# Modulation vectors of a transformer block: shift and scale made among the attention's units, the gate around the selection, loads in that order

## The chip, the cores and the metric

The kernel runs on one core of a Trainium2 chip. The metric is the device time of one execution in microseconds; the runs shown are of the whole program, inputs in HBM, result written back to HBM. Its engines are TensorE (PE; PEld is its weight load), VectorE (DVE), ScalarE (ACT), GpSimd (POOL) and SyncE (SP), which here only issues DMAs. Each engine runs its own list of instructions in order; semaphores order them against each other.

## The reference

A first block (gated recurrence and a dilated attention) is followed by a second block of two layers. All of it is float32. The second block is what the change touches, cut to its shape here:

```python
for i in range(2):
    m  = (silu(c)     @ w_ada[i] + b_ada[i]).reshape(1, 1, 6, 1024)   # six vectors for the 512 tokens
    mc = (silu(c_ctx) @ w_ada[i] + b_ada[i]).reshape(6, 1024)         # and for the 256 context tokens
    h  = rmsnorm(x) * g * (1 + m[1]) + m[0]                           # shift 0, scale 1
    y  = even_mixer(...) if i == 0 else odd_mixer(...)                # attention and projection
    x  = x + m[2] * y                                                 # gate 2
    h  = rmsnorm(x) * g2 * (1 + m[4]) + m[3]                          # shift 3, scale 4
    x  = x + m[5] * ec_moe(h)                                         # gate 5
# ec_moe: softmax over 16 experts; each expert takes its 64 best tokens (32 of the context);
#         y = (silu(xs @ w_gate) * (xs @ w_up)) @ w_down, times the router's value, added back
```

In layer 0 the same is done for the context, with `mc`. Layer 1 is the last and has no context behind its attention. `w_ada[i]` is 1024 x 6144, so each of the six vectors is a product of two rows (token and context) with a 1024 x 1024 matrix of 4 MB; each expert's three matrices are 4 MB each, 16 experts a layer.

## The kernel before

The program is written once per engine. `tensor()`, `vector()`, `scalar()`, `gpsimd()` and `sync()` list the stages in order: first block, `even` projection of layer 0, attention `ea` (24 differential pairs, 48 units), attention `eb` (48 units), output projection `oute`, `moe(0)`, the `odd` projection, attention `o` (64 units), output projection `outo`, `moe(1)`.

Weights pass through slots of 16 KB a partition in the arena `AR`: slots 0 and 1 are always free for them, slots 2 to 5 lie over the memory of the stages and slot 6 over the residual rows. `LOADS` is one list in the order in which SyncE issues the loads, 2 MB each as a rule; `sync()` walks it. Before it issues a load it waits until the slot's last content has been used (`slot_freed`) and, for some keys, for more. SyncE also writes the normalised rows (`h_rows`) and residual rows (`x_rows` or `out`) to HBM in `sp_moe`, and reads `x_rows` back before the `odd` norm. Because SyncE runs in order, a wait for one slot holds all loads behind it.

A vector `(l, j)` (layer, number; layer -1 is the first block) is made in these steps. `pe_ada_mm` multiplies the two input rows with one half of the matrix: eight matmuls of 512 columns with weights 32 wide, in turn in the four column groups of the array (L407). `dve_ada_row` copies the half to `RB1` (L440), or adds the bias where the vector is a gate (L438, `j` 2 or 5). `pe_ada_end` then turns the row into columns with eight small matmuls (L426), or, for a gate, spreads it over the partitions with matmuls against `sel` (L421), and `dve_ada_end` writes the columns to `MC` and `MG` (L467, L475) or the gate to `GB` (L454). `RB1` is one buffer, so the vectors are made one after the other.

In the first attention (`AT1`) such work already runs as fill: `Attn` takes a list of items, spread over its units, and each engine runs the items of unit `i` four steps later. `fine(l, j)` cuts a vector into eight items of two matmuls, an empty item and `ada_end`. `pe_attn`, `dve_attn` and `act_attn` serve `ea`; `pe_pairs` and its like serve `eb` and `o`, where the fill holds the `up` groups of the next heads. In both, `pe_scores` is L632, the turn of the probabilities L643, the product with the values L667 or L843, the maximum L732, the exponential L687.

`moe(l)` before: PE makes vectors 3 and 4 (`pe_ada(l, 3)`, `pe_ada(l, 4)`), turns the normalised rows and routes them (L541, L1826), serves the selection (`pe_topk`; the selection itself is a row of `max`, `max_index` and `match_replace` on DVE, L1896 to L1900), makes vector 5, turns the indices (`pe_idx`), in layer 0 makes vector 0 of layer 1, and goes to the experts. DVE has the same order: norm, 3, 4, `dve_hT`, `dve_topk`, 5, `dve_idx` (L1918 to L1926), and `dve_ada(1, 0)` in layer 0. GpSimd gathers an expert's rows (L2234) once the indices are there and scatters the result with an add (L2247). In layer 0 every weight is split into two parts first (ACT L1943, DVE L1951, matmuls L1985); in layer 1 the matmuls read it as it is (L2170).

Of the kernel before, what the change touches and what calls it, by code (L numbers as in the profile page):

```python
# [153 lines left out]
def program(nc, T, out, known):  # L154
    ctx = ExitStack()
    with ctx:
# [4 lines left out]
        K = Banks(P, C)  # L161
# [92 lines left out]
        def colchunk(key, w, n0, n1, slots):  # L254
            cyc(key, w[:, n0:n1].rearrange("(c p) n -> p c n", p=128), (w.shape[0] // 128, n1 - n0), slots)

        three, two, four, six = [0, 1, 2], [0, 1], [0, 1, 2, 6], [0, 1, 2, 3, 4, 5]

# [26 lines left out]
        for i, (a, b) in enumerate(EVEN_CH):  # L285
            colchunk(("even", i), T["w_in_even_2"][0], a, b, two)
        for i in range(2):
            colchunk(("oute", i), T["w_out_even_2"][0], i * 512, i * 512 + 512, two)
        ada_loads(0, [3, 4], two)
        ada_loads(0, [5], three)  # L290
        ada_loads(1, [0], three)
        expert_loads(0)
        ada_loads(1, [1, 2], three)
        colchunk(("odd",), T["w_in_odd_2"][0], 0, 416, two)
        add(("qup",), T["w_q_up_2"][0].rearrange("(c p) n -> p c n", p=128), (2, 1536), 0)
        add(("kvup",), T["w_kv_up_2"][0], (1, 2048), 1)
        rr[0] = 0
        for i in range(2):
            colchunk(("outo", i), T["w_out_odd_2"][0], i * 512, i * 512 + 512, two)
        ada_loads(1, [3, 4], two)  # L300
        ada_loads(1, [5], three)
        expert_loads(1)
# [347 lines left out]
        def pe_attn(A, fill=None):  # L650
            n = len(A.units)
            for step in range(n + 4):
                if step < n:
                    pe_scores(A, step)
                i = step - 2
                if 0 <= i < n and not A.units[i].get("skip"):
                    pe_turn_p(A, i)
                i = step - 3
                if 0 <= i < n and not A.units[i].get("skip"):
                    u = A.units[i]  # L660
                    nn = u["nk"] // 128
                    b = K.fill(6 + (i // 2 if A.mixed else i) % 2, "pv", A.tag, i)
                    P.wait_ge("read", "tr", A.tag, i)
                    u["vready"](P)
                    ptc = A.Pt[i % len(A.Pt)]
                    for k in range(nn):
                        m = pe.matmul(bank(b)[:, 0:128], ptc[:, 128 * k:128 * k + 128], u["v"](k), start=(k == 0),  # L667
                                      stop=(k == nn - 1))
                    m.then_inc(*K.full("pv", A.tag, i))
                i = step - 4  # L670
                if 0 <= i < n:
                    for it in A.fill[i]:
                        fill(it)
# [1036 lines left out]
        for j in range(6):  # L1710
            k0, nk = (0, 768) if j < 4 else (512, 256)
            for h in range(4):
                for c in range(2):
# [3 lines left out]
                                      out=O6[:, j, 128 * h:128 * h + 128], skip=(c == 0), mix=(c == 1)))  # L1717
        ATA = Attn("ea", units, Pb4, PTb)
        units = []
# [14 lines left out]

        def pe_fillB(it):
            pass

# [193 lines left out]
        def act_split(l, i):  # L1931
            if i >= len(PIECES[l]):
                return
            key, hf = PIECES[l][i]
            if i < 3:
                S.wait_ge("full", MLAST[l], 1, OUTP[MLAST[l]] - 1)
            elif i < 4:
                S.wait_ge("xw", l)
                S.wait_ge("read", MLAST[l], 1, OUTP[MLAST[l]] - 1)
            else:  # L1940
                S.wait_ge("used", l, i - 4)
            weight_wait(S, key)
            s.copy(pair(i)[0], raw_half(key, hf)).then_inc(*S.up("hi", l, i))  # L1943
# [327 lines left out]
        def dve_moe(l):  # L2271
            tag = f"m{l}"
            res_wait(V, MLAST[l])
            dve_norm(tag)
            dve_ada(l, 3)
            dve_ada(l, 4)
            dve_hT(tag)
            dve_topk(l)
            dve_ada(l, 5)
            dve_idx(l)  # L2280
            if l == 0:
                dve_ada(1, 0)
            dve_experts1() if l else dve_experts(l)

        def pe_moe(l):
            pe_ada(l, 3, 7)
            pe_ada(l, 4, 6)
            pe_route(l)
            pe_topk(l)
            pe_ada(l, 5, 7)  # L2290
            pe_idx(l)
            if l == 0:
                pe_ada(1, 0, 7)
            pe_experts1() if l else pe_experts(l)
# [279 lines left out]
        for gi in range(4):  # L2574
# [13 lines left out]
            if gi < 3:  # L2588
                for i in range(13):
                    fills.setdefault(max(0, 16 * gi - 2 + i), []).append(("up", gi + 1, i))  # L2590
        ATO = Attn("o", units, Pb4, [GB[0], GB[2], GB[3]], fills=fills, Rb=RbA)
        norm_mem("m1")


        def tensor():
# [13 lines left out]
            pe_even()  # L2609
            pe_attn(ATA)  # L2610
            pe_pairs(ATB, pe_fillB)
            pe_oute()
            pe_moe(0)
            pe_ada(1, 1, 6)
            pe_ada(1, 2, 7)
            pe_hT("no")
            pe_odd()
            for i in range(13):
                pe_up(0, i)
            pe_pairs(ATO, lambda it: pe_up(it[1], it[2]))  # L2620
            P.wait_ge("read", "pv", "o", 63)
# [3 lines left out]
        def vector():  # L2625
# [24 lines left out]
            V.wait_ge("full", "hturn", *HTS[-1])  # L2650
            dve_attn(ATA)
            V.wait_ge("full", "pv", "ea", 47)
# [3 lines left out]
            dve_outproj("oute", OT, gsc, tmps, 0)  # L2656
            dve_moe(0)
            dve_ada(1, 1)
            V.wait_ge("xr", 0)
# [5 lines left out]
            for i in range(13):  # L2665
                dve_up(0, i)
            dve_pairs(ATO, lambda it: dve_up(it[1], it[2]))
            dve_outproj("outo", OT4, None, tmps, 1)
            dve_moe(1)

        def scalar():
# [24 lines left out]
            S.wait_ge("full", "even", 4, 5)  # L2696
            act_attn(ATA)
            S.wait_ge("full", "pv", "ea", 47)
# [10 lines left out]
            for i in range(13):  # L2709
                act_up(0, i)  # L2710
            act_pairs(ATO, lambda it: act_up(it[1], it[2]))
            act_outproj("outo", OT4, None)
            act_moe(1)

        def gpsimd():
# [9 lines left out]
            for i in range(13):  # L2725
                pool_up(0, i)
            pool_pairs(ATO, lambda it: pool_up(it[1], it[2]))
            pool_outproj("outo", tmps)
            pool_experts(1)

        def sync():
            for i, (key, src) in enumerate(LOADS):
# [4 lines left out]
                if key[0] == "ada" and key[3] == 1 and key[2] in (2, 5):  # L2737
                    sp_bias(key[1], key[2])
                if key == ("ada", 1, 0, 1):
                    sp_moe(0)  # L2740
                if key == ("gate", 1, 0, 1):
                    sp_moe(1)
                if key == ("ada", 1, 2, 1):
                    Q.wait_ge("scat", 0, 15)
                    sp.dma_start(XALL, T["x_rows"].rearrange("(j p) d -> p j d", p=128))\
                        .then_inc(*Q.up("xr", 0, by=16))
                if slot == 2 and key[0:2] in (("ada", 0), ("ada", 1)) or key[0:2] in (("gate", 0), ("up", 0)):
                    Q.wait_ge("full", "oute", 1, 5)
                if slot == 6:
                    Q.wait_ge("xw", 0)  # L2750
                if slot >= 2 and key[0:3] == ("ada", 1, 5) or key[0:2] in (("gate", 1), ("up", 1)):
                    Q.wait_ge("full", "pv", "o", 63)
# [46 lines left out]
```

## Time and profile before

| | us |
|---|---|
| median of 3 runs (2689.45 to 2700.64) | 2689.82 |
| profiled execution, its own time | 2695.25 |
| its span in the profile | 2693.7 |
| PE busy in the span | 2309.2 (86%) |
| DVE busy | 1314.5 (49%) |
| ACT busy | 982.1 (36%) |

The page's line on the chain that ended last gives PE 50%, DVE 18%, DMA 17%, ACT 9% and "issue" 5% of the span. Where the stages lie in the profiled execution, by the starts of their rows:

| stage | from | to |
|---|---|---|
| attention `ea` | 636 | 750 |
| attention `eb` | 750 | 868 |
| projection `oute` | 868 | 951 |
| between, layer 0 | 951 | 1055 |
| experts of layer 0 | 1055 | 1640 |
| between the layers, `odd` | 1640 | 1767 |
| attention `o` | 1767 | 2056 |
| projection `outo` | 2056 | 2111 |
| between, layer 1 | 2111 | 2191 |
| experts of layer 1 | 2191 | 2694 |

A row of a timeline or a chain begins with its start and its duration in us; what stands in square brackets is the idle time of that engine before it and who ended it. An idle engine costs nothing unless it is on the chain.

### The profile page before, as it was taken

Reading aid. Unit: us, or ns where it says so; the run is one execution under the profiler, and the core shown is the slowest. Engines: PE = TensorE matmul, PEld = TensorE weight load, DVE = VectorE, ACT = ScalarE, POOL = GpSimd, SP = SyncE. Lnnn points to the kernel's source line nnn. Section 1 sums busy time; section 2 is a strip of 40 time slices with the busy share of each in tenths; the row PEclk is TensorE's granted clock in tenths of the full one; section 3 lists DMA queues with packets and bytes.
Section 4 is the critical chain, followed back from the end, with each engine's and each line's share of the span. In section 5 each row is a group of like instructions: output and inputs, shape, how many; then the busy total and the mean of one; then the engine's idle time right before and its main releaser. Section 6 shows DMA issues by size and latency. Waiting matters only on the chain.

```text
span 2693.7 us, 26540 instructions
## 1 busy us (share of the span) xinstructions
PE 2309.2 (86%) x10239; PEld 1279.2 (47%) x10239; DVE 1314.5 (49%) x2428; ACT 982.1 (36%) x1612; POOL 389.3 (14%) x324
## 2 busy tenths in 40 slices
PE   4998987999899985999999996778889868777787
PEld 2444533446666433666676663445555322222222
DVE  2147525536864135998888893466663131111111
ACT  2014333214554024888888872244442100000000
POOL 0000000000111100255445520000001001000000
PEclk9999998999999977999999996889999879999999
DMA  7113501101000077999999986000010689999998
GB/s 261 63 63 107 184 22 67 63 16 63 1 1 2 31 282 288 337 372 365 369 380 372 373 347 232 18 1 1 1 63 13 244 343 400 402 402 405 406 412 343
DMA packets 92347, 546.31 MB, mean 203 GB/s; under 512 B 7711, under 2 KB 10543, under 8 KB 67518
## 3 DMA queue, kind: packets, MB, share of 16 engines
q1 hardware_dynamic: 81806, 518.95, 49.2%
q0 software_dynamic: 6144, 20.98, 3.4%
q10 hardware_dynamic: 4272, 4.69, 0.5%
q8 instruction: 82, 1.34, 0.2%
q14 instruction: 43, 0.35, 0.0%
HBM read 523.62 MB, written 20.97 MB: 202 GB/s over the span
## 4 chain that ended last, share of the span: by engine, by line
PE 50%; DVE 18%; DMA 17%; ACT 9%; issue 5%; ACTq 0%; POOL 0%; SPq 0%; DVEq 0%; POOLq 0%
DMA AR<-in_w_exp_gate_dram 13%; PE PS L1610 7%; DVE RW L1951 6%; PE PS L632 6%; PE PS L930 5%; PE PS L1985 5%; PE PS L2170 4%; PE PS L643 3%; ACT AR L2039 3%; PE PS L1317 3%; ACT RW L1943 2%; PE PS L1151 2%; PE PS L843 2%; PE PS L407 2%; PE PS L667 1%
## 5 line engine op out<-in xcount | busy, mean ns | idle before, releaser
L1951 DVE TENSOR_TENSOR RW<-AR,RW 128x2048 fp32r<-128x2048 f32 x192 | 432.2, 2283 | 54.3 <-ACT RW L1943 54.3
L2170 PE MATMUL PS<-AR 128*64 128x512 f32 x1536 | 375.6, 636 | 94.8 <-DMA AR<-in_w_exp_gate_dram 47.4
L1943 ACT CAST RW<-AR 128x2048 fp32r<-128x2048 f32 x192 | 363.8, 1912 | 145.4 <-PE PS L1985 108.2
L1985 PE MATMUL PS<-RW,RX 128*96 128x512 f32 x1536 | 364.0, 396 | 15.7 <-DVE RX L2084 15.2
L1985 PEld LDWEIGHTS PS<-RW,RX 128*96 128x96 f32 x1536 | 248.4, 163 | 122.2 <-issue 16.3
L2170 PEld LDWEIGHTS PS<-AR 128*64 128x64 f32 x1536 | 115.0, 145 | 330.1 <-issue 261.9
L632 PE MATMUL PS<-AR 128*128 128x256 f32 (+5 forms) x640 | 243.9, 498 | 4.4 <-POOL AR L617 2.3
L1610 PE MATMUL PS<-AR 128*128 128x512 f32 (+1 forms) x480 | 193.5, 560 | 3.4 <-DMA AR<-in_w_in_even_dram 3.4
L1985 PE MATMUL PS<-RW,RA 128*96 128x512 f32 x768 | 185.4, 397 | 11.7 <-DVE RA L2118 11.7
L732 DVE TENSOR_REDUCE AR<-PS 128x1 f32<-128x768 f32 (+1 forms) x160 | 135.6, 847 | 88.4 <-PE PS L632 88.1
L2247 POOL DMA_INDIRECT x_rows<-AR x16 | 119.3, 7458 | 352.2 <-DVE AR L2128 278.0
L2234 POOL DMA_INDIRECT AR<-h_rows,AR x32 | 146.1, 4566 | 164.9 <-DVE AR L1922 77.6
L2187 ACT COPY AR<-PS 128x512 f32<-128x512 f32 x16 | 9.4, 587 | 410.4 <-PE PS L2155 410.4
L632 PEld LDWEIGHTS PS<-AR 128*128 128x128 f32 (+1 forms) x640 | 110.4, 196 | 102.2 <-issue 96.3
L687 ACT ACTIVATE AR<-PS,AR 128x768 f32<-128x768 f32 (+1 forms) x160 | 130.6, 816 | 70.4 <-DVE AR L732 28.2
L1985 PEld LDWEIGHTS PS<-RW,RA 128*96 128x96 f32 x768 | 123.1, 163 | 68.4 <-issue 17.2
L930 PE MATMUL PS<-AR 128*128 128x512 f32 x320 | 137.8, 593 | 1.1 <-DVE AR L953 0.6
L1610 PEld LDWEIGHTS PS<-AR 128*128 128x128 f32 x480 | 91.3, 194 | 93.3 <-issue 91.1
L643 PE MATMUL PS<-AR 128*128 128x128 f32 x800 | 118.0, 277 | 20.2 <-ACT AR L709 7.5
L617 POOL COPY AR<-AR 64x128 f32<-64x128 f32 x80 | 25.4, 322 | 705.3 <-ACT AR L1650 313.3
L407 PE MATMUL PS<-AR 128*32 128x512 f32 x480 | 86.7, 786 | 44.5 <-DMA AR<-in_w_ada_dram 31.2
L643 PEld LDWEIGHTS PS<-AR 128*128 128x128 f32 x800 | 94.4, 142 | 62.2 <-issue 15.9
(328 smaller groups left out, 2672.1 us busy)
## 6 DMA issues: line engine op xcount, KB each, us to landing
AR<-in_w_exp_gate_dram SPq DMA_DIRECT2D x64, 2048.0 KB, 14.2
AR<-in_w_exp_up_dram SPq DMA_DIRECT2D x64, 2048.0 KB, 11.1
AR<-in_w_exp_down_dram SPq DMA_DIRECT2D x64, 2048.0 KB, 21.8
AR<-in_w_ada_dram SPq DMA_DIRECT2D x30, 2048.0 KB, 8.2
AR<-in_w_in_dram SPq DMA_DIRECT2D x6, 2048.0 KB, 8.2
AR<-in_w_in_even_dram SPq DMA_DIRECT2D x4, 2048.0 KB, 8.2
AR<-in_w_out_dram SPq DMA_DIRECT2D x2, 2048.0 KB, 8.6
AR<-in_w_out_even_dram SPq DMA_DIRECT2D x2, 2048.0 KB, 7.8
```

What stands on the lines that cost most here:

```text
L407: m = pe.matmul(bank(b)[c0:c0 + 32, :], (sl if l < 0 else sl2)[:, k, :], w[:, k, :], start=(k < 4), stop=(k >= 4), tile_position=(0, c0))
L632: m = pe.matmul(PS[:, p0 + a // 512, 0:e_ - a], q, u["k"][:, a:e_], start=True, stop=True)
L643: m = pe.transpose(PS[:, 4 + k // 4, 128 * (k % 4):128 * (k % 4) + 128], pc[:, 128 * k:128 * k + 128], ident)
L687: ex = s.activation(pc[:, 0:nk], pc[:, 0:nk] if A.masked else psf[:, 512 * p0:512 * p0 + nk], ACT.Exp, bias=A.mx[:, i % 8:i % 8 + 1], accu ...
L732: v.tensor_reduce(nm, sc_, AX, ALU.max, negate=True).then_inc(*V.up("mx", A.tag, i))
L930: m = pe.matmul(bank(b), OT[:, c, 128 * j:128 * j + 128], w[:, c, :], start=(c == 0), stop=(c == 7))
L1610: m = pe.matmul(bank(b)[:, 0:a1 - a0], HT6[:, k, 128 * j:128 * j + 128], w[:, k, :], start=(k == 0), stop=(k == 7))
L1943: s.copy(pair(i)[0], raw_half(key, hf)).then_inc(*S.up("hi", l, i))
L1951: v.tensor_tensor(lo, raw_half(key, hf), hi.bitcast(F32), ALU.subtract).then_inc(*V.up("split", key, hf))
L1985: m = pe.matmul(bank(ob)[0:Mc, :], st_, mv[:, k, 512 * q_:512 * q_ + 512], start=(k0 + k == 0 and n_ == 0), stop=(k0 + k == 7 and n_ == 2))
L2170: m = pe.matmul(bank(b)[64 * q_:64 * q_ + 64, :], op, w[:, c, 512 * q_:512 * q_ + 512], start=(h == 0 and c == 0), stop=(h == 1 and c == 3 ...
L2234: g.indirect_dma_start(xs[e % 3], None, T["h_rows"], bass.IndirectOffsetOnAxis(ap=IDX[0:R, e:e + 1], axis=0))\
```

## The change

- Vectors 3 and 4 of layer 0 become fill of `ea`, one item in each of units 1 to 20, all in PSUM bank 7; `pv` of `ea` uses bank 6 alone. Vectors 3 and 4 of layer 1 become fill of `o`, units 44 to 63. They leave `moe(l)`.
- Vector 5: its matmuls and row adds come first in `moe(l)`, its end steps (`ada_end`) behind `pe_idx` and `dve_idx`.
- Vector 0 of layer 1 moves from before the experts of layer 0 to behind them, where vectors 1 and 2 are made.
- The loads follow: `ada(0, 3)` and `ada(0, 4)` ahead of `oute`; `ada(0, 5)` in slots 4 and 5 once `eb` has ended; the experts' slots start over at slot 0; `ada(1, 3)` and `ada(1, 4)` ahead of and between the two loads of `outo`, whose first goes to slot 3; `ada(1, 5)` in slots 2 and 4; layer 1's six slots in another order.
- On SyncE, `sp_moe(0)` now stands before the fourth expert load, `sp_moe(1)` before the seventh, and the read of `x_rows` before `odd` instead of before the second half of `ada(1, 2)`.
- The second and third split of layer 0 on ScalarE wait until vector 5's matmuls have read slots 4 and 5.

```diff
-        three, two, four, six = [0, 1, 2], [0, 1], [0, 1, 2, 6], [0, 1, 2, 3, 4, 5]
+        three, two, four, six = [0, 1, 2], [0, 1], [0, 1, 2, 6], [5, 1, 2, 4, 3, 0]
...
+        ada_loads(0, [3, 4], two)
         for i in range(2):
             colchunk(("oute", i), T["w_out_even_2"][0], i * 512, i * 512 + 512, two)
-        ada_loads(0, [3, 4], two)
-        ada_loads(0, [5], three)
-        ada_loads(1, [0], three)
+        rr[0] = 0
+        ada_loads(0, [5], [4, 5])
+        rr[0] = 0
         expert_loads(0)
-        ada_loads(1, [1, 2], three)
+        rr[0] = 0
+        ada_loads(1, [0, 1, 2], three)
         colchunk(("odd",), T["w_in_odd_2"][0], 0, 416, two)
...
-        for i in range(2):
-            colchunk(("outo", i), T["w_out_odd_2"][0], i * 512, i * 512 + 512, two)
-        ada_loads(1, [3, 4], two)
-        ada_loads(1, [5], three)
+        ada_loads(1, [3], two)
+        colchunk(("outo", 0), T["w_out_odd_2"][0], 0, 512, [3])
+        rr[0] = 0
+        ada_loads(1, [4], two)
+        colchunk(("outo", 1), T["w_out_odd_2"][0], 512, 1024, [0])
+        rr[0] = 0
+        ada_loads(1, [5], [2, 4])
+        rr[0] = 0
         expert_loads(1)
...
-                    b = K.fill(6 + (i // 2 if A.mixed else i) % 2, "pv", A.tag, i)
+                    b = K.fill(6 + (0 if A.mixed else i % 2), "pv", A.tag, i)
...
-        ATA = Attn("ea", units, Pb4, PTb)
+        ATA = Attn("ea", units, Pb4, PTb, fill=[("none",)] + fine(0, 3) + fine(0, 4))
...
+        def pe_fill_ada(it):
+            if it[0] == "ada":
+                pe_ada_mm(it[1], it[2], it[3], 7, it[4], it[4] + 2)
+            if it[0] == "ada_end":
+                pe_ada_end(it[1], it[2], 7)
+
+        def dve_fill_ada(it):
+            if it[0] == "ada" and it[4] == 6:
+                dve_ada_row(it[1], it[2], it[3])
+            if it[0] == "ada_end":
+                dve_ada_end(it[1], it[2])
...
                 S.wait_ge("full", MLAST[l], 1, OUTP[MLAST[l]] - 1)
+                if i:
+                    S.wait_ge("full", "ada", l, 5, i - 1)
...
             dve_norm(tag)
-            dve_ada(l, 3)
-            dve_ada(l, 4)
+            dve_ada_row(l, 5, 0)
+            dve_ada_row(l, 5, 1)
             dve_hT(tag)
             dve_topk(l)
-            dve_ada(l, 5)
             dve_idx(l)
-            if l == 0:
-                dve_ada(1, 0)
+            dve_ada_end(l, 5)
             dve_experts1() if l else dve_experts(l)
...
-            pe_ada(l, 3, 7)
-            pe_ada(l, 4, 6)
+            pe_ada_mm(l, 5, 0, 7)
+            pe_ada_mm(l, 5, 1, 6)
             pe_route(l)
             pe_topk(l)
-            pe_ada(l, 5, 7)
             pe_idx(l)
-            if l == 0:
-                pe_ada(1, 0, 7)
+            pe_ada_end(l, 5, 7)
             pe_experts1() if l else pe_experts(l)
...
+        for i, it in enumerate(fine(1, 3) + fine(1, 4)):
+            fills.setdefault(44 + i, []).append(it)
...
             pe_moe(0)
+            pe_ada(1, 0, 7)
             pe_ada(1, 1, 6)
             pe_ada(1, 2, 7)
...
-                if key == ("ada", 1, 0, 1):
+                if key == ("up", 0, 0, 1):
                     sp_moe(0)
-                if key == ("gate", 1, 0, 1):
+                if key == ("down", 1, 0, 0):
                     sp_moe(1)
-                if key == ("ada", 1, 2, 1):
+                if key == ("odd",):
                     Q.wait_ge("scat", 0, 15)
                     sp.dma_start(XALL, T["x_rows"].rearrange("(j p) d -> p j d", p=128))\
                         .then_inc(*Q.up("xr", 0, by=16))
-                if slot == 2 and key[0:2] in (("ada", 0), ("ada", 1)) or key[0:2] in (("gate", 0), ("up", 0)):
+                if key[0:3] == ("ada", 0, 5):
+                    Q.wait_ge("full", "pv", "eb", 47)
+                if key[0:2] in (("gate", 0), ("up", 0)):
                     Q.wait_ge("full", "oute", 1, 5)
...
+                if key == ("outo", 0):
+                    Q.wait_ge("full", "pv", "o", 47)
-                if slot >= 2 and key[0:3] == ("ada", 1, 5) or key[0:2] in (("gate", 1), ("up", 1)):
+                if key[0:3] == ("ada", 1, 5) or key[0:2] in (("gate", 1), ("up", 1)):
                     Q.wait_ge("full", "pv", "o", 63)
```

`pe_ada(1, 0)` and `dve_ada(1, 0)` are called behind `moe(0)` on both engines; `pe_attn(ATA)`, `dve_attn(ATA)` and the `o` pairs are given the fill functions.

## Rows read from the trace of the kernel before

**Rows 1.** Chain in order of time, attention `ea`: start, us, what.
```profile
657.26 1.58 PE PS L667 x12
...
662.19 1.58 PE PS L667 x12
```
**Rows 2.** Windows: length, busy us (instructions) of PE, PEld, DVE, ACT, POOL; clock, DMA, GB/s.
```profile
1200.00:1500.00 300.00, 293.99 (x1333) 208.46 (x1332) 269.87 (x177) 245.62 (x268) 153.38 (x17) 1.00 1.00 373
1985.00:2056.00 71.00, 63.70 (x525) 46.17 (x523) 40.21 (x93) 33.87 (x64) 3.25 (x11) 1.00 0.17 61
```
**Rows 3.** Chain, last steps of attention `o`.
```profile
2048.86 0.92 ACT AR L863
```
**Rows 4.** Timeline of SyncE's queue, experts of layer 1: start, us, instruction.
```profile
2197.83 0.33 SPq L2756 DMA_DIRECT2D AR<-in_w_exp_down_dram  x1
```
**Rows 5.** Chain, layer 1 from the first gather, and its last load landed.
```profile
2182.58 5.70 DMA AR<-h_rows,AR
...
2678.37 8.79 PE PS L2170 x32
```
**Rows 6.** Chain, first attention, whose fill holds vectors.
```profile
258.83 1.00 PE PS L407 x8
...
286.96 1.70 PE PS L426 x16
```
**Rows 7.** Timeline of PE behind the experts of layer 0.
```profile
1639.94 3.64 PE L407 MATMUL PS<-AR 128*32 128x512 f32 x32
...
1663.47 3.64 PE L407 MATMUL PS<-AR 128*32 128x512 f32 x16 [14.67 <-DMA AR<-in_w_ada_dram]
```
**Rows 8.** Timeline between the even projection and the experts of layer 0.
```profile
961.05 3.23 ACT L507 ACTIVATE AR<-AR 128x1024 f32<-128x1024 f32 x3 [0.84 <-DVE AR L362]
...
978.70 1.52 PE L541 MATMUL PS<-AR 128*128 128x128 f32 x6 [0.31 <-issue]
...
982.29 2.74 PE L1826 MATMUL PS<-AR 128*16 128x512 f32 x4
...
999.92 0.68 DVE L1870 COPY AR<-PS 16x512 f32<-16x512 f32 x1 [1.68 <-PE PS L1826]
...
1022.65 1.28 DVE L438 TENSOR_TENSOR AR<-AR,PS 128x512 f32<-128x512 f32 x2
...
1028.91 0.69 DVE L454 COPY AR<-PS 96x512 f32<-96x512 f32 x1 [2.11 <-PE PS L421]
...
1030.71 1.12 POOL L2234 DMA_INDIRECT AR<-h_rows,AR  x1 [77.64 <-DVE AR L1922]
...
1046.47 4.49 DVE L1951 TENSOR_TENSOR RW<-AR,RW 128x2048 fp32r<-128x2048 f32 x2 [3.62 <-ACT RW L1943]
...
1053.72 0.96 DVE L2084 TENSOR_TENSOR RX<-AR,RX 128x768 fp32r<-128x768 f32 x1 [2.76 <-ACT RX L2048]
1054.94 13.85 PE L1985 MATMUL PS<-RW,RX 128*96 128x512 f32 x48 [15.17 <-DVE RX L2084]
```
**Rows 9.** Chain behind the experts of layer 0: last scatter, then the residual rows.
```profile
1642.20 5.29 DMA x_rows<-AR
...
1647.51 10.42 DMA AR<-x_rows
```
**Rows 10.** DMA issues by line: KB each, median us from issue to landing.
```profile
x_rows<-AR POOLq DMA_INDIRECT x16, 17.2
```
**Rows 11.** Timeline between the odd projection and the experts of layer 1.
```profile
2119.35 2.19 ACT L507 ACTIVATE AR<-AR 128x1024 f32<-128x1024 f32 x2 [0.83 <-DVE AR L362]
...
2138.76 1.77 PE L541 MATMUL PS<-AR 128*128 128x128 f32 x8 [0.31 <-issue]
...
2174.65 1.27 DVE L438 TENSOR_TENSOR AR<-AR,PS 128x512 f32<-128x512 f32 x2
```
**Rows 12.** Windows of 4 us in the turns and routing of layer 0, columns as in Rows 2.
```profile
980.00:984.00 4.00, 3.42 (x11) 1.46 (x10) 1.56 (x2) 1.13 (x2) 0.00 (x0) 0.50 1.05 387
984.00:988.00 4.00, 4.00 (x18) 1.95 (x17) 0.81 (x1) 0.56 (x1) 0.00 (x0) 0.83 1.05 389
```

More of the change, by code:

```diff
@@ L1733, in program @@
         sq = AR[:, H0 + 4608:H0 + 5120]
-        def pe_fillB(it):
-            pass
+        def pe_fill_ada(it):
[8 more added lines that the diff above has]
+                dve_ada_end(it[1], it[2])
         def act_fillB(it):
@@ L2609, in tensor @@
             pe_even()
-            pe_attn(ATA)
-            pe_pairs(ATB, pe_fillB)
+            pe_attn(ATA, pe_fill_ada)
+            pe_pairs(ATB, lambda it: None)
             pe_oute()
             pe_moe(0)
+            pe_ada(1, 0, 7)
             pe_ada(1, 1, 6)
@@ L2619, in tensor @@
                 pe_up(0, i)
-            pe_pairs(ATO, lambda it: pe_up(it[1], it[2]))
+            pe_pairs(ATO, lambda it: pe_up(it[1], it[2]) if it[0] == "up" else pe_fill_ada(it))
             P.wait_ge("read", "pv", "o", 63)
@@ L2650, in vector @@
             V.wait_ge("full", "hturn", *HTS[-1])
-            dve_attn(ATA)
+            dve_attn(ATA, dve_fill_ada)
             V.wait_ge("full", "pv", "ea", 47)
@@ L2657, in vector @@
             dve_moe(0)
+            dve_ada(1, 0)
             dve_ada(1, 1)
@@ L2666, in vector @@
                 dve_up(0, i)
-            dve_pairs(ATO, lambda it: dve_up(it[1], it[2]))
+            dve_pairs(ATO, lambda it: dve_up(it[1], it[2]) if it[0] == "up" else dve_fill_ada(it))
             dve_outproj("outo", OT4, None, tmps, 1)
@@ L2696, in scalar @@
             S.wait_ge("full", "even", 4, 5)
-            act_attn(ATA)
+            act_attn(ATA, lambda it: None)
             S.wait_ge("full", "pv", "ea", 47)
@@ L2710, in scalar @@
                 act_up(0, i)
-            act_pairs(ATO, lambda it: act_up(it[1], it[2]))
+            act_pairs(ATO, lambda it: it[0] == "up" and act_up(it[1], it[2]))
             act_outproj("outo", OT4, None)
@@ L2726, in gpsimd @@
                 pool_up(0, i)
-            pool_pairs(ATO, lambda it: pool_up(it[1], it[2]))
+            pool_pairs(ATO, lambda it: it[0] == "up" and pool_up(it[1], it[2]))
             pool_outproj("outo", tmps)
```

## The prediction

> **What bounds the kernel now.** I read the page's forty slices first, then the chain that ended last in order of time, then windows and timelines where the change acts. Four stages matter, with different limits.
> In the even layer's first attention the chain is TensorE alone: its pattern of two units repeats from 657.26 to 662.19, 4.93 us, gapless but for 0.12 us [rows 1]. In the odd layer's attention PE is busy 63.70 of 71.00 us [rows 2], and the chain leaves it only in the last steps, where it waits for ScalarE (0.92 us here, and a second time at 2053.16) [rows 3]. So work given to PE in either attention is paid in full, unless it falls into those last steps.
> Layer 0's experts are bound by PE, DVE and ACT together (293.99, 269.87 and 245.62 of 300 us) [rows 2]. Layer 1's are bound by loads: the first slot comes free at 2197.83 [rows 4], and 90 of the 96 loads come after it until 2678.37 [rows 5], 480.5 / 90 = 5.34 us each. In either case the stage keeps its length, and what counts is when it starts.
>
> **The even attention pays.** The change puts the shift and scale vectors of layer 0 into attention `ea`, as 16 items of two matmuls and two end steps. The same items are in the first attention of before: an item takes 1.00 us of the chain there (its neighbours 0.98 to 1.00; I take 0.99), an end 1.70 [rows 6]. 16 x 0.99 + 2 x 1.70 = 19.2 us. In one block the same matmuls cost half: two halves of a vector, 32 instructions, take 3.64 us [rows 7], against 7.9 in eight items. VectorE's copies of the rows (0.69 us each) fall at the end of an even step, just before a wait for scores that the item itself has put back, so they cost nothing; waited for in full, four would cost 2.8 us. Lower bound: items at a block's price, 11 us; upper: the clock at half throughout, 35. I take **+19.2**, since [rows 6] show the same items in the same kind of loop.
> The Trainium skill ("TensorE: Matmul & The Clock Gate", Part 3: Packing small matmuls) says that matmuls on different column groups run concurrently and gives 2.38 times for three groups. An item fills two of four, so by that it is about one matmul long, and a block half as dear: the rows agree with it.
> The single PSUM bank for `pv` costs nothing: PE's next `pv` already waits for a DVE copy that stands behind the read of the last one in DVE's order. The projection's own two loads go behind four others, but are issued by the middle of `ea` and needed two attentions later.
>
> **Between attention and experts in layer 0.** Before, PE makes vectors 3 and 4 from loads that only start when the projection ends, and turns the first column at 978.70; the normalised rows are ready at 961.05 + 3.23 = 964.28 [rows 8]. After, vector 5's halves are loaded during the projection and multiplied while the norm runs, so the turn starts at 964.4: 14.3 us sooner. Turns, routing and selection keep their length. Behind the selection, before: row adds from 1022.65, gate vector ended by the copy at 1028.91 + 0.69 = 1029.60, first gather at 1030.71 [rows 8]. After, the 1.1 us of index work follow directly: gather at 1022.65 - 14.3 + 1.1 = 1009.4, 21.3 sooner. It needs h_rows written. That write and x_rows', 6 MB, now stand behind three expert loads issued at 951: six pieces of 2 MB in all, 951 + 2.4 + 6 x 5.34 = 985, in time (2.4: below). The gather lands 5.70 us later, as in layer 1 [rows 5], at 1015.1. ScalarE has the tokens scaled by about 1021. DVE is what is late: end of the gate vector, 5.5 us as before without the row adds, to 1014.6; four splits at 2.24; 0.96 for the tokens, and 0.3 to PE: 1014.6 + 9.0 + 0.96 + 0.3 = 1024.9, against 1054.94 [rows 8]. **-30.0 us.** Should the gather take the median of 12.1, -25.6. Vector 0 of layer 1, which also stood here, moves behind the experts; that is in the -30.0.
>
> **Behind the experts of layer 0: a loss.** Before, the residual rows are loaded at 1647.51, right when the last scatter lands, into an empty queue: 10.42 us [rows 9]. PE waits for the load issued next until 1663.47 [rows 7], 5.5 us after the rows landed, so loads of this queue land one behind the other at its rate; and 10.42 less one and a half loads of 5.34 leaves 2.4 of latency. After, SyncE issues the row load last, behind three loads of `ada` whose slots PE frees only after the experts: the first at 1639.94 + 1.82 = 1641.8, the second at 1643.6, the third about 1648.3 (3.64, a copy, an end step and half a vector after 1639.94). They land at 1649.5, 1654.8 and 1660.2, and the rows, 8.0 us more, at 1668.2 instead of 1657.93: +10.3. The last scatter took 5.29 us alone [rows 9] and takes 17.2 in the median, beside loads [rows 10]; now two loads run beside it, so it may land at 1659.4 rather than 1647.5, which only takes its own 0.4 MB out of the queue's time. I take **+11**, bounds 0 (the rows not held up) and +14. The norm, vector 2 and the turn hang on this load, in the same order as before. `kvup` behind `qup` is hidden: 2.4 + 6.7 for the two, and PE gets to it 11 us after they are issued.
> By the Trainium skill ("DMA: Bandwidth & Descriptors", Queues, rings and completion order) descriptors of a ring are taken in order, but a later one may finish its write first. If that mattered, the rows could be complete before the third load; the 5.5 us behind the row load speak for plain order.
>
> **The odd attention pays too.** Another 19.2 us, less two waits of about 1.0 in the last steps and 0.4 before the projection [rows 3]: **+16.8**. Its first load is issued when the up groups end and is needed five steps later, 12 us if a step took no more than half of 4.93, against 2.4 + 5.3 = 7.7: hidden. Were it not, 5 us.
>
> **Between attention and experts in layer 1.** The turn can start when the rows are ready, 2119.35 + 2.19 = 2121.6, not at 2138.76: -17.2. From the row adds at 2174.65 to the gather at 2182.58 are 7.9 us, of which 0.9 stay: -7.0 [rows 5, 11]. The rest of the gate vector (5.5) lies beside the gather's 5.70. Together -24.1. The expert loads, now from the attention's end on, fill the same six slots, which were full in time before; nothing of their head start reaches the end. Here the turn now starts on a cold clock, where the blocks of `ada` had brought it back before, so I give back 2: **-22.1**.
>
> **Sum.** +19.2 - 30.0 + 11 + 16.8 - 22.1 = -5.1 us. Against the profiled execution's own 2695.25 (span 2693.7) that is 2690.1. The runs shown have a median of 2689.82, so 2684.7.
>
> **Rivals.**
> (a) The row load is not held up by the three in front of it. Sum -16.1: 2673.7. For: SyncE issues them without waiting for a landing. Against: the 5.5 us above.
> (b) The items are cheaper than in the first attention, as PE's next matmuls slip into the two free column groups: at 0.6 us, 32 x 0.39 = 12.5 less: 2672. Against: there too the next matmul started only after 1.00 us [rows 6].
> (c) Slower, by the clock. TensorE's granted clock was 0.50 (1.2 GHz) at 980 to 984 and came back, 0.83 in the next 4 us, while turns and routing kept PE busy [rows 12]. Before, matmuls of `ada` stood ahead of the turns; now 7 to 10 us of idleness do. If the clock stayed down through all eight columns, each would take 1.52 + 2.74 = 4.3 us, 34 in place of the 21 from 978.70 to 999.92 [rows 8]: +13 here, and about +9 in layer 1, of which 2 are counted: 2704.7. It decides when PE idles so long in each column that the clock is not given back; the 4.00 busy of 4.00 us at 984 speak against it.
> (d) The gain in layer 0 doesn't arrive whole: the gather takes 12.1 us, or ScalarE's fourth split waits for x_rows. Up to +5: 2690.
> (e) The change doesn't hide what it means to hide: a load in an attention is late and PE stands, 5 to 10 us: 2692.
>
> **Chances.** Forecast 0.45; (a) 0.15; (b) 0.10; (c) 0.08; (d) 0.12; (e) 0.10. Half a per cent, 13.4 us, is about what a measurement of this kernel can tell from no change. (a) and (b) lie just beyond it: faster 0.26. (c) and the worst of (e) are slower: 0.10. Same: 0.64. The range reaches from below both cheap cases, 2669, to 2700, past (e) and short of (c).
>
> **What would show it.** Right: `ea` 19 us longer; first expert matmul of layer 0 some 11 us sooner than 1054.94; 45 us instead of 34 from PE's last work on those experts to its next turn; the odd attention 17 us longer; in layer 1 the first gather 37 us behind the normalised rows instead of 61. Wrong: a row load that lands within 12 us of the scatter, items much shorter than 0.9 us, or a granted clock of 0.50 through the turns.

## The result

The changed kernel takes 2703.34 us (median), the kernel before 2692.30 us beside it on the same chip: ratio 1.0042, 95% interval 1.0028 to 1.0055. It is slower by 11 us where 5 us less were predicted, and 2703.3 lies outside the range of 2669 to 2700. The profiled execution of after has a span of 2701.6 us, before 2693.7. Two of the kernels below (the even part undone, the gate part alone) were profiled in an execution far slower than their others, so only the times of the others are used for them.

Most of what was predicted is in the profile, in the predicted places. What isn't, is the price in the attentions. The table gives each stretch of both profiled executions, from the start of one row of PE's timeline to the start of the next.

| stretch | before | after | difference | predicted |
|---|---|---|---|---|
| start to attention `ea` | 635.8 | 640.5 | +4.7 | 0 |
| `ea` and `eb`, to the first matmul of the projection | 232.6 | 257.6 | **+25.0** | +19.2 |
| projection to first turn | 110.3 | 96.1 | -14.2 | -14.3 |
| first turn to first expert matmul, layer 0 | 76.2 | 59.7 | -16.5 | -15.7 |
| experts, scatter, row load, to the first turn of `odd` | 619.1 | 631.7 | +12.6 | +11 |
| that turn to attention `o` | 93.1 | 89.6 | -3.5 | 0 |
| attention `o` | 289.1 | 314.4 | **+25.3** | +16.8 |
| projection, turn, to first expert matmul, layer 1 | 135.1 | 112.8 | -22.3 | -22.1 |
| experts of layer 1 | 502.5 | 499.1 | -3.4 | 0 |
| span | 2693.7 | 2701.6 | +7.9 | -5.1 |

Three rows of it (+4.7, -3.5, -3.4) are stretches in which PE's work did not change. They show how far one execution strays from the next (the kernels profiled below have 634 to 645, 87 to 90 and 500 to 504 us there), and with them why 11 us between the medians need not be 7.9 between the profiles.

The chain in attention `ea` of after answers to [rows 1] (L673 is L667 of before) and [rows 6] (L413 is L407, L432 is L426). Columns: start, us, what.

```profile
676.46 0.98 PE PS L413 x4
677.45 1.49 PE PS L638 x4
...
684.81 1.58 PE PS L673 x12
686.38 3.62 PE PS L432 x16
690.01 2.77 PE PS L638 x4
692.78 0.87 PE PS L649 x6
693.65 0.98 PE PS L413 x4
694.63 1.49 PE PS L638 x4
```

An item is 0.98 us, as predicted. The end step is 3.62 us, not 1.70, and the scores behind it take 2.77 us where the next ones take 1.49. The windows of that place say why (length, busy us of PE, PEld, DVE, ACT, POOL, granted clock, DMA share, GB/s): the clock is whole through most of the end, falls to 0.50 of full speed just before the end is over, and is whole again by 694. The last line shows one us of it. PE was busy 3.88 to 4.00 of 4.00 us all along.

```profile
684.00:688.00 4.00, 3.88 (x23) 3.41 (x22) 3.07 (x6) 2.77 (x5) 0.29 (x1) 1.00 1.05 403
688.00:692.00 4.00, 4.00 (x12) 2.96 (x13) 0.17 (x1) 0.00 (x0) 0.00 (x0) 0.71 0.08 29
692.00:696.00 4.00, 4.00 (x17) 2.17 (x17) 2.21 (x5) 1.69 (x3) 0.29 (x1) 0.86 0.00 0
...
690.00:691.00 1.00, 1.00 (x3) 0.48 (x3) 0.17 (x1) 0.00 (x0) 0.00 (x0) 0.50 0.00 0
```

Attention `o` has the same ends, and the waits for ScalarE of [rows 3] are still there, just ahead of the last of them. Timeline of PE:

```profile
2048.03 3.68 PE L432 MATMUL PS<-AR 128*128 128x2 f32 x16
...
2084.41 1.53 PE L849 MATMUL PS<-AR 128*64 128x128 f32 x24 [1.14 <-ACT AR L869]
2085.87 3.90 PE L432 MATMUL PS<-AR 128*128 128x2 f32 x16
2089.62 2.91 PE L936 MATMUL PS<-AR 128*128 128x512 f32 x3
```

Between attention and experts, layer 0, for [rows 8]: PE is idle for 9.85 us before the turn (L547). The profile names the row adds of vector 5 (L444), which end at 994.07; the normalised rows end at 994.03, so the turn starts as soon as they are there, as predicted, and waits for no shift or scale. In layer 1 the row adds end 0.4 us behind the rows. Layer 1, for [rows 11] and [rows 5]: turn at 2156.93, gather at 2194.01, 37.1 us apart and, as predicted, 37 behind the normalised rows.

```profile
994.18 1.53 PE L547 MATMUL PS<-AR 128*128 128x128 f32 x6 [9.85 <-DVE AR L444]
...
2156.93 1.95 PE L547 MATMUL PS<-AR 128*128 128x128 f32 x8 [7.10 <-DVE AR L444]
...
2194.01 0.98 POOL L2251 DMA_INDIRECT AR<-h_rows,AR  x1 [45.67 <-DVE AR L1933]
```

The chain behind the experts of layer 0, for [rows 9]:

```profile
1640.15 9.43 DMA x_rows<-AR
1649.60 19.96 DMA AR<-x_rows
1669.58 6.35 ACT AR L508 x12
```

### The profile page after: what moved, and what is told of

Read it like the earlier page. It is cut to its first block, busy times and chain, and to the rows that moved or that the text cites. A ratio compares the mean times of both kernels' runs of the same rounds, so it can differ in the third digit from the quotient of the medians.

```text
span 2701.6 us, 26538 instructions
## 1 busy us (share of the span) xinstructions
PE 2316.3 (86%) x10239; PEld 1283.7 (48%) x10239; DVE 1315.9 (49%) x2428; ACT 982.4 (36%) x1612; POOL 398.6 (15%) x324
## 4 chain that ended last, share of the span: by engine, by line
PE 50%; DVE 18%; DMA 16%; ACT 9%; issue 5%; ACTq 0%; POOL 0%; SPq 0%; DVEq 0%; POOLq 0%
DMA AR<-in_w_exp_gate_dram 13%; PE PS L1616 7%; DVE RW L1968 7%; PE PS L638 6%; PE PS L936 5%; PE PS L2002 5%; PE PS L2187 4%; PE PS L649 3%; ACT AR L2056 3%; PE PS L1323 3%; ACT RW L1960 2%; PE PS L413 2%; PE PS L1157 2%; PE PS L849 2%; PE PS L673 1%
## 5 line engine op out<-in xcount | busy, mean ns | idle before, releaser
L2187 PE MATMUL PS<-AR 128*64 128x512 f32 x1536 | 365.4, 621 | 101.5 <-DMA AR<-in_w_exp_gate_dram 49.0
L2251 POOL DMA_INDIRECT AR<-h_rows,AR x32 | 155.6, 4862 | 117.2 <-DVE AR L1937 55.9
L936 PE MATMUL PS<-AR 128*128 128x512 f32 x320 | 139.3, 598 | 0.6 <-DVE AR L959 0.6
L649 PE MATMUL PS<-AR 128*128 128x128 f32 x800 | 119.9, 280 | 19.2 <-ACT AR L715 7.5
L1616 PEld LDWEIGHTS PS<-AR 128*128 128x128 f32 x480 | 91.3, 194 | 93.1 <-issue 90.9
L623 POOL COPY AR<-AR 64x128 f32<-64x128 f32 x80 | 25.3, 322 | 736.5 <-ACT AR L1656 313.0
L1323 PE MATMUL PS<-AR 128*128 128x512 f32 x256 | 111.8, 592 | 0.0
```

The costliest lines, as they stand in the source:

```text
L649: m = pe.transpose(PS[:, 4 + k // 4, 128 * (k % 4):128 * (k % 4) + 128], pc[:, 128 * k:128 * k + 128], ident)
L936: m = pe.matmul(bank(b), OT[:, c, 128 * j:128 * j + 128], w[:, c, :], start=(c == 0), stop=(c == 7))
L1323: m = pe.matmul(bank(b), HT4[:, k, 128 * j:128 * j + 128], w[:, k, :], start=(k == 0), stop=(k == 7))
L1616: m = pe.matmul(bank(b)[:, 0:a1 - a0], HT6[:, k, 128 * j:128 * j + 128], w[:, k, :], start=(k == 0), stop=(k == 7))
L2187: m = pe.matmul(bank(b)[64 * q_:64 * q_ + 64, :], op, w[:, c, 512 * q_:512 * q_ + 512], start=(h == 0 and c == 0), stop=(h == 1 and c == 3 ...
L2251: g.indirect_dma_start(xs[e % 3], None, T["h_rows"], bass.IndirectOffsetOnAxis(ap=IDX[0:R, e:e + 1], axis=0))\
```

## Experiments

Each ratio is to the kernel before, measured beside it (medians 2690.65 to 2690.97 us). A difference between two such ratios is known to some 0.0018, or 5 us.

**Ends with contiguous weights.** The end of vectors 3 and 4 takes every fourth column of `RB1` as weights (`perm(k)`), that of vectors 0 and 1 (the ends of [rows 6]) takes 128 columns in a row. Stored in the end's order, the rows of 3 and 4 can be read in the same way:

```diff
-  RB1[:, perm(k) if j > 2 else slice(128 * k, 128 * k + 128)]
+  RB1[:, 128 * k:128 * k + 128]
...
 # in dve_ada_row
+  elif j in (3, 4):
+      v.tensor_copy(dst.rearrange("p (r i) -> p i r", r=4), src.rearrange("p (i r) -> p i r", r=4))
```

> The kernel after, but VectorE stores the rows of vectors 3 and 4 in the order in which the end step reads them, so that the eight small matmuls of an end take contiguous weights instead of every fourth column. After the change an end of vector 3 or 4 takes 3.62 us where the prediction had 1.70, and the scores behind it run at a granted clock of 0.50. Theory S (the strided weights are the price): the four ends in the two attentions fall to 1.7 to 1.9 us, 7.7 us in all, and the dip of the clock stays: ratio to before 1.001 (after: 1.004). Theory S+ (the dip hangs on the length of the slow block too): another 6 us, ratio 0.999. Theory P (it is the place, the clock or the wait that makes 3.62 of 1.70, not the stride): ends stay at 3.6, ratio 1.004.

Ratio 1.0003 (0.9991 to 1.0015), 10.5 us below after: S, and most of S+. Chain of this kernel at the same end (L641 are the scores, L652 the turn), and its window:

```profile
679.40 1.58 PE PS L676 x12
680.97 1.68 PE PS L432 x16
682.65 1.40 PE PS L641 x4
684.05 0.65 PE PS L652 x6
684.71 0.98 PE PS L413 x4
```
```profile
684.00:688.00 4.00, 4.00 (x24) 2.46 (x23) 2.99 (x6) 1.93 (x3) 0.58 (x2) 1.00 0.00 0
```

An end is 1.68 us and nothing behind it is slow. What changed is the load of the weights. Groups by line of the two stretches, after first (busy us, mean ns of one):

```profile
L432 PEld LDWEIGHTS PS<-AR 128*128 128x128 f32 x16 | 3.8, 328 | 0.0
```
```profile
L432 PEld LDWEIGHTS PS<-AR 128*128 128x128 f32 x16 | 1.9, 192 | 0.0
```

328 ns for a load of 128 columns 16 bytes apart, 192 ns for contiguous ones. The loads keep PE's load side busy through the whole of either end (3.8 and 1.9 us), so they set its length. The Trainium skill ("SBUF — State Buffer", Door 1: The DMA port swizzle) says that consecutive accesses to one line of 16 bytes go at full bandwidth and that each access which goes to a new line pays a penalty; the stride that it gives as free for float32 is 4. At a stride of four elements, 16 bytes, each column lies in a line of its own. The rows agree with the penalty, and they put four itself on the paying side.

In this profile `ea` with `eb` take 250.5 us, 17.9 more than before, against +19.2 predicted with an end of 1.70.

**One matmul of eight in an end.** `for k in range(7 if j > 2 else 0, 8)`. The kernel leaves out seven eighths of each of these vectors; it is there for the price alone.

> The kernel after, but the end steps of vectors 3 and 4 do one of their eight small matmuls; seven columns of eight of the shift and scale are left out (old PSUM contents in their place). It gives the whole price of an end in an attention, what follows it included. If an end costs 3.62 alone: 3.2 us less each, four of them 12.7 us, ratio to before 0.9995. If the drop of the clock behind it belongs to it: 1.6 us more each, 19 us in all, ratio 0.997, and no granted clock of 0.50 behind the ends. By the prediction's price (1.70 us for an end): 6 us, ratio 1.002.

Ratio 0.9969 (0.9956 to 0.9982): 19.6 us below after for four ends, 4.9 each. So an end as after has it costs 3.62 less what is left of it, and the slow stretch behind. Behind this kernel's ends the scores take 1.54 us in the timeline, in after 2.91.

**Pieces of an end, weights as in after.** Wide items as in the next run, and the end cut into four pieces of two matmuls, each in a unit of its own: `for k in range(k0, k0 + 2)`.

> The kernel with wide items, with strided weights as in after, but an end is cut into four pieces of two small matmuls, one piece to a unit. The matmuls and their weights stay; only the unbroken stretch of them is gone. Theory D (the drop of the granted clock behind an end comes from the long stretch of slow small matmuls): no 0.50 behind the pieces, a piece of 0.9 us, 3.6 for an end as before, and the 1.3 to 2.5 us behind each end gone: 5 to 10 us below the wide kernel's ratio of 0.9996, so 0.997. Theory R (the drop is the engine's activity over much longer time, not this stretch): the ratio stays at 0.9996, and each piece costs something more: up to 1.002.

Ratio 0.9959 (0.9946 to 0.9972), 10 us below the wide kernel: D. Its chain:

```profile
666.55 0.83 PE PS L433 x4
667.37 1.40 PE PS L640 x4
668.77 0.66 PE PS L651 x6
669.43 0.83 PE PS L433 x4
670.25 1.40 PE PS L640 x4
```

The four pieces cost 3.3 us together, little less than an unbroken end, but behind none of the eight pieces in `ea` does a slow stretch follow: the scores stay at 1.40 and the clock at 1.00. Of the gain, 1.2 us lie in the ends themselves (four times 3.62 less 3.32) and some 6 in the slow rows behind them (1.37 for the scores and 0.21 for the turn, four times). So it was the unbroken stretch of slow, two-column matmuls that brought the clock down in `ea`, with PE counted as busy throughout. Pieces don't rule it out: in attention `o` of this kernel two pieces stand 1.5 us apart (at 2049.34 and 2050.88), and the clock is 0.50 from about 2053 to 2055, where the product with the values takes 2.77 us instead of 1.53. What brought it down there wasn't isolated. Timeline:

```profile
2050.88 0.99 PE L433 MATMUL PS<-AR 128*128 128x2 f32 x4
2052.09 1.25 PE L651 MATMUL PS<-AR 128*128 128x128 f32 x6 [0.22 <-ACT AR L871]
2053.28 2.77 PE L851 MATMUL PS<-AR 128*64 128x128 f32 x24
```

**Wide items.** Four matmuls to an item instead of two, 16 items in place of 32: `pe_ada_mm(..., it[4], it[4] + 4)`.

> The kernel after, but an item in the attentions holds four matmuls (all four column groups) instead of two, so there are 16 items in place of 32; in the odd attention they run from unit 48 on. Theory G (an item costs what its slowest column group costs, whatever stands in the others): a wide item takes the 1.0 us of a narrow one, 16 us less, ratio to before 0.998. Theory I (what costs is each instruction, 0.5 us): a wide item takes 2.0 us, nothing changes, ratio 1.004.

Ratio 0.9996 (0.9983 to 1.0009), 12.4 us below after: G. A wide item takes 0.99 us in the chain of the later kernel with all repairs (below), a narrow one 0.98:

```profile
654.12 0.99 PE PS L413 x8
655.11 1.49 PE PS L641 x4
```

The trace of before already showed it. Two instructions are one matmul here, so a row with x8 in its first attention is a unit that holds two items, in all four column groups, and a row with x4 a unit with one:

```profile
261.56 0.99 PE PS L407 x8
...
264.40 0.98 PE PS L407 x4
```

Of the 16 us, `ea` with `eb` show only 4.1 and `o` 3.4 in this execution. The 8 us that `ea` saves are there up to the last end; some 4 go again where `ea` passes to `eb` and PE idles in every unit: the clock is 0.83 at 760 to 780 us, where after has 1.00. One profiled execution of each can't tell whether that belongs to the kernel. The window in this kernel, then in after:

```profile
760.00:780.00 20.00, 16.01 (x60) 9.37 (x59) 11.70 (x35) 7.99 (x22) 2.73 (x7) 0.83 0.00 1
```
```profile
760.00:780.00 20.00, 14.29 (x68) 8.67 (x67) 12.87 (x43) 9.24 (x27) 3.30 (x8) 1.00 0.00 1
```

**Rows earlier.** `if key == ("ada", 1, 2, 1)` for the row load in place of `("odd",)`.

> The kernel after, but the load of the residual rows stands ahead of the last load of vector 2 of layer 1, as it did before, not behind it. Theory Q (the prediction's: loads of this queue land one behind the other): the rows have two loads in front of them instead of three, land 5 to 7 us sooner than 20 us after the last scatter, and the squares of the odd norm end 23 to 25 us behind the scatter's start instead of 29.4; ratio to before 1.002. Theory W (the last load of vector 2, now behind the rows, is what PE then waits for): squares sooner, but the first turned column of the odd norm not; ratio 1.004. Theory B (bandwidth is shared, order does not matter): rows land as late as before, ratio 1.004.

Ratio 1.0019 (1.0005 to 1.0033), 6.2 us below after: Q. Chain:

```profile
1645.72 8.50 DMA x_rows<-AR
1654.24 14.48 DMA AR<-x_rows
```

Three loads in front: 19.96 us. Two: 14.48, so the third costs 5.5. None: 10.42 [rows 9], so the two others cost 4.1 together. That is less than 5.5 each: they were issued 7 and 9 us ahead of the rows, the third, in after, 2.7 us ahead. What counts is how much of them is still to land. By the stage table's measure, experts to turn is 624.8 us in place of 631.7.

**The odd part undone.** Vectors 3 and 4 of layer 1 are made in `moe(1)`; the rest of the change stays.

> The kernel after, but vectors 3 and 4 of layer 1 are made behind attention o and its projection as before, with their loads there and ahead of the first expert loads; the rest of the change stays. It prices the odd part alone. By the profiled stages of after (attention 25.4 us longer, projection 1.3, the stretch to the experts 23.6 shorter, end of the expert loads 3.3 later) that part costs 6: without it ratio to before 1.002. By the prediction it brings 5.3: without it ratio 1.006.

Ratio 1.0037 (1.0019 to 1.0054): the odd part costs 1 us, give or take 6. Its profile: attention `o` 291.2 us (23.2 less), projection to turn 88.2 (20.9 more: vector 5's products now stand there too), experts of layer 1 503.7. In the profiles the price in the attention and the gain behind it cancel.

**The even part undone.** The same for layer 0.

> The kernel after, but vectors 3 and 4 of layer 0 are made behind the projection as before; the rest of the change stays. It prices the even part alone. By the profiles so far: attentions ea and eb with the projection's start 25 us shorter; from the projection to the turn 14 us longer as before and 5 to 6 more, because vector 5's halves stand there too (the kernel with the odd part undone showed 88.2 us there, before 82.6): 20 us; so 5 us less in sum, ratio to before 1.0023. By the prediction's own terms (19.2 against 14.3 and the halves of vector 5, 3.6): 1 us less, ratio 1.0038.

Ratio 1.0035 (1.0015 to 1.0056): the even part costs 2 us, give or take 6; the two values expected aren't told apart.

**Contiguous weights in the kernel before.** The edit of the first run alone.

> The kernel before with the contiguous weights of the first run alone: VectorE stores the rows of vectors 3 and 4 in the order of the end step. If the strided weights are the price wherever they stand, the two ends ahead of the turns fall from 3.86 to 1.9 us in either layer; all four are on the path (PE goes from the last of them to the turn with 0.31 us idle), so 7.7 us or a little more, ratio 0.997. If the first end of each pair is hidden behind the load of the next vector: 3.8 us, ratio 0.9985. If the stride costs only within an attention: 1.000.

Ratio 1.0004 (0.9991 to 1.0016): a miss for all but the last, whose condition (the stride costs only within an attention) isn't what the trace shows. Timeline of PE and chain of this kernel:

```profile
968.24 3.64 PE L407 MATMUL PS<-AR 128*32 128x512 f32 x16 [6.18 <-DMA AR<-in_w_ada_dram]
974.31 3.54 PE L426 MATMUL PS<-AR 128*128 128x2 f32 x16 [2.43 <-DVE AR L440]
977.79 5.25 PE L407 MATMUL PS<-AR 128*32 128x512 f32 x32
984.28 1.92 PE L426 MATMUL PS<-AR 128*128 128x2 f32 x16 [1.25 <-DVE AR L440]
```
```profile
2180.41 9.40 DMA AR<-h_rows,AR
```

Only the second end of a pair gets cheap. The first stands behind 6.18 us of idleness, the granted clock is 0.50 there, and at half clock contiguous weights take 3.54 us. VectorE's permuted copies are dearer (1041 ns in the mean, 687 before), four times on the path. The first column of the turns, directly behind the cheap end, runs at a whole clock (0.96 us in layer 0, where before has 1.52 [rows 8]). So 1.4 and 2.0 us were won up to the turns. In layer 1 of this execution the first gather landed 9.40 us after its issue instead of 5.70 [rows 5], which ate them; whether other executions do the same isn't known. In an attention, where the clock is whole and the copies are beside the path, the same edit was worth 10.5.

**All three repairs.** Contiguous ends, wide items, rows ahead of the last load.

> Three edits of the first runs together in the kernel after: rows of vectors 3 and 4 stored so that the ends read contiguous weights (worth 10.5 us alone), items of four matmuls (12.4 us), the residual rows loaded ahead of the last load of vector 2 (6.2 us). If they act in different places and add up: 11.3 - 10.5 - 12.4 - 6.2 = 17.8 us below before, ratio 0.9934. If they share a gain (the drop of the clock, which the contiguous ends and perhaps the wide items too keep away): a third less, ratio 0.996.

Ratio 0.9907 (0.9890 to 0.9924), 2668.54 us: the gains add up, and this kernel beats both. Attentions `ea` and `eb` are 13.8 us longer than before and `o` 12.2, while the stretches behind them keep their gains: 157.2 us from projection to experts in layer 0 (before 186.5), 111.3 in layer 1 (135.1). Row load of 13.56 us:

```profile
1628.43 9.42 DMA x_rows<-AR
...
1637.87 13.56 DMA AR<-x_rows
```

**Rows ahead of both loads.** `if key == ("ada", 1, 2, 0)` in the last kernel.

> The kernel with all three repairs (0.9907), but the residual rows are loaded ahead of both loads of vector 2 of layer 1, so behind one load instead of two. Theory Q (one behind the other): the rows land 5 us sooner; vector 2 then lands 10.6 us behind them and PE has 3.6 us of matmuls and the gate's end to make before it turns, so about 3 of the 5 arrive: ratio 0.9895. Theory W (vector 2 sets the turn by then): ratio 0.9907, and PE waits for the last load of vector 2 longer than before.

Ratio 0.9907 (0.9890 to 0.9925): W. In the profile the squares start 18.7 us after the last scatter's start, in the kernel before this one 23.0; but PE waits until 1660.79 for vector 2's second half and turns at 1667.8, 39.1 us behind its first work on vector 0 against 40.4. The rows are no longer what is late. With one load in front they landed after 10.3 us, no later than with none: that load had all but landed when they were issued.

**The gate part alone.** Vectors 3 and 4 of both layers behind the projections, contiguous ends, rows ahead of the last load.

> The gate part alone, with the two repairs that don't need the attentions: vectors 3 and 4 of both layers behind the projections (contiguous weights), vector 5's products ahead of the turn and its end behind the selection, vector 0 of layer 1 behind the experts, the residual rows loaded ahead of the last load of vector 2. Against the kernel with all three repairs (ratio 0.9907) it tells whether the attentions are still the right place once the price there is down. Theory A (they are): 14 and 12 us in the attentions are given back, but 14 to 20 us in front of each turn come back: 10 us above it, ratio 0.9945. Theory N (nothing is won by the place, only by the gate around the selection and the rows): ratio 0.991.

Ratio 0.9967 (0.9952 to 0.9983): A. Between this kernel and the one with all repairs lie 16 us, known to 6, so A's 10 just fits: that is what the place is worth once an item and an end are cheap. The place was right; it was what was put there that was dear.

The kernels with parts undone don't add up. From after to this kernel are 20 us (1.0042 to 0.9967). The earlier rows account for 6, the two parts undone one by one for 3, contiguous weights behind the projections for nothing that could be measured. Some 10 us are left without a cause, out of differences known to 5 or 6 each.

## Why the prediction was wrong

**The step that failed is the price of an end in the attentions.** The prediction took 1.70 us for it from [rows 6], "since [rows 6] show the same items in the same kind of loop". For an item that held, though the row cited, x8, is one of two items. The ends are not the same, as vectors 3 and 4 read their weights with a stride. The trace of before had them too, a few rows further on, in the very stretch that the change empties:

```profile
964.47 3.86 PE L426 MATMUL PS<-AR 128*128 128x2 f32 x16 [1.60 <-DVE AR L440]
968.26 5.34 PE L407 MATMUL PS<-AR 128*32 128x512 f32 x32
974.52 3.86 PE L426 MATMUL PS<-AR 128*128 128x2 f32 x16 [0.91 <-DVE AR L440]
```

With 3.62 for 1.70 and 1.3 for the slow scores behind, an end costs 3.2 more. Four of them: 13 us, and 10.5 were measured for taking this away. That alone turns -5.1 into +5 to +8.

**The drop of the clock behind an end** was not in the sum. Rival (c) looked for it in the turns, after idleness. It came in the attention, with PE fully busy. Before's trace had it, just ahead of the rows that (c) cites: the clock is 1.00 through the strided end at 974.52, with PE busy for 3.78 of 3.80 us, and 0.50 from 978.7 on, where the turn begins ([rows 12] have the next 4 us). At 288.91, behind the row cited for an end, an item takes 1.80 us as well; that one is chance, since the kernel of the first experiment has the same work in the same place and 1.05 us.

**Even attention**, +19.2: right with its own price of an end (17.9 measured with contiguous ends). **Odd attention**, +16.8: 19.7 with contiguous ends. The 2.4 us to be hidden in the last steps weren't; the wait of 1.14 us for L869 in the result's rows stands ahead of the item and remains.

**Layer 0 between**, -30.0: measured -30.7, both halves right (-14.2 and -16.5). Rival (c) is false: the turn started on a low clock, which was back by the third column (0.99 us at 1000.38), about as soon as in before. Rival (d) did not occur. **Layer 1 between**, -22.1: measured -22.3, and that close by luck. Of its two terms, the gain behind the turn came whole (-7.0) and the one ahead of it short (-15.3 for -17.2). The 2 us given back for a cold turn were not lost there: the turn of before starts at a low clock too (0.60 at 2138.7 to 2140.7). 1.4 us were lost where the projection starts, at 0.50 behind the last end (L936 in the result's rows), and 0.4 by the row adds. With contiguous ends, projection to turn takes 65.9 us in place of 67.3.

**Row load**, +11: measured +12.6 to the turn, by the mechanism given, loads of one queue landing one behind the other (5.5 us for the last in front, by the run with the rows earlier). The rows landed 13.7 us later behind the last scatter's start than before; the scatter itself, beside the loads, took 9.43 us instead of 5.29, and the rows are issued only when it has landed. Rival (a) is false.

**Rival (b)**, cheaper items, is false as such (0.98), but its sentence on free column groups pointed to what wide items then brought. **Rival (e)** did not occur; no load in an attention was late.

Of "what would show it", `ea` was 25 us longer, not 19; the first expert matmul 1.1 us sooner, not 11, of which 4.7 us lie ahead of `ea` and 5.8 in the ends; 47.7 us from PE's last expert work to its next turn where 45 were said (1637.9 to 1685.6); `o` 25 us longer, not 17; 37 us to the gather, as said. The sum had a margin of 5 us and hung on a gain of 52 against a loss of 47, so a mis-sized 13 decided its sign. The range left out exactly this.

The attribution of 11 us to single causes rests on differences known to 5 us each. That ends, items and row load each cost time, about as much as the runs say, is shown; the split of an end's price into load time (1.9 us) and clock (1.3) rests on the profiles.

## What to carry to other kernels

Cost a moved instruction by the rows of that very instruction, with its operands' strides, in the stretch where it stands now; a row of its namesake elsewhere is no substitute. Before work is put between others in an engine that is full there, make it as short as it can be: fill all column groups, read weights contiguously, and don't let narrow matmuls run on unbroken. And when a list of loads is reordered, look for the one that something waits for at once: here a load of 2 MB issued just ahead of it cost 5.5 us, one issued long before it next to nothing, and after one step something else was late.

## What was not expected of the hardware

- A load of 128 columns of float32 weights takes 192 ns contiguous and 328 ns at a stride of 16 bytes, at a whole clock. At half clock an end of eight took 3.54 us contiguous, at a whole clock 1.92 (the kernel before with contiguous weights). Strided it took 3.86 us at either: in the kernel before the clock is 0.50 through the end at 964.47 and 1.00 through the one at 974.52. The strided load gains nothing from the faster clock.
- An unbroken 3.6 us of two-column matmuls was followed by a granted clock of 0.50 with PE 3.9 to 4.0 of 4.0 us busy; cut into pieces of 0.83 us with some 2 us of other matmuls between them it was not, with two pieces starting 1.5 us apart it was once. An unbroken 1.7 us was followed by it once, in the first attention of before, and not in the same place in the first experiment. What exactly makes the difference isn't settled.
- Four matmuls on the four column groups took 0.99 us, two took 0.98.
